# Interleaving two narrow projections with their neighbours, folding the squares of four norms, and moving work in two attention stages of a two-block transformer on one core

## The chip, the cores and the metric

The kernel runs on one core of one Trainium2 chip. The metric is the device time of the whole program in microseconds, the median of several runs. The engines of the core are written as in the profile: PE (TensorE), DVE (VectorE), ACT (ScalarE), POOL (GpSimd) and SP (SyncE, which here issues the DMAs of the weights).

## The reference

Batch 1, 256 positions, width 1024. The first block has two layers. Cut to what matters here, layer 1 is

```python
hk = rmsnorm(x, kv_norm_g)
kvf = hk @ kvf_w                                    # keys 1024, values 1024, 16 forget gates
k, v = kvf[..., :D], kvf[..., D:2 * D]
log_f = log_sigmoid(kvf[..., 2 * D:] + fgate_b)
c_bhs = cumsum(log_f, axis=1)
x = x + fox_attention(rmsnorm(x, norm_mix_g[1]), w_q, w_o, k, v, c_bhs)
x = x + memory_cross_attention(rmsnorm(x, norm_mem_g[1]), mem_n, ...)
x = x + square(relu(rmsnorm(x, norm_ff_g[1]) @ ff_w1)) @ ff_w2
```

and the second block (`mod = silu(c) @ w_ada + b_ada`, a product with a 1024 x 9216 matrix, gives its nine shifts, scales and gates) is

```python
u = modulate(rmsnorm(h, norm_ff1), sh1, sc1)
h = h + 0.5 * g1 * ((silu(u @ w_gate) * (u @ w_up)) @ w_down)
u = modulate(rmsnorm(h, norm_mix), sh2, sc2)
gq, gk, gv, glr, gog, mq, mk, mv, ga, gb = split(u @ w_in)      # glr is 16 wide
log_a = log_sigmoid(glr @ w_gla_lr + b_gla_lr) / 16
y_a = (rmsnorm(gla_chunked(gq, gk, gv, log_a)) * silu(gog)) @ w_br_gla
y_b = moba_attention(mq, mk, mv, rel_bias) @ w_br_moba
h = h + g2 * ((sigmoid(ga) * y_a + sigmoid(gb) * y_b) @ w_out)
# then a second gated feed-forward, and a last rmsnorm
```

## The kernel before

Everything is held transposed: `x` is 8 tiles (kt) of 128 features by 256 positions, taken in 4 pairs p. Every product with a weight matrix is a **stage** of **chunks** (the table in `plan`), mostly 1024 x 256 of weights. A value is split into a high half (rounded) and a low half (the rest), and each product is high x high, low x high and high x low, so a tile pair costs a matmul 128x512 (L452) and one 128x256 (L454).

Each chunk goes round a ring of 4 slots: SP loads it to `raw`, ACT writes its high half (`split_hi`, L1062) 4 chunks ahead, DVE its low half (`split_lo`, L1588) 3 chunks ahead, PE multiplies into one of two accumulators `acc`, ACT copies the low part out (`low`, L1072), DVE adds it (`total`, L1602). PE may start a chunk when both halves of its weights are there (`weights_ready`) and the chunk two before it is summed (`acc_free`). The order on every engine is written by hand: each engine's block calls the same stages, and `leads` and `between` put chunks among the heads of an attention.

**Norms.** After a residual stage (`residual` on PE and ACT, `add_to_x` on DVE) ACT squares each pair of `x` into `aux` (two slots, L1109, the last pair tile by tile, L1198), PE sums over the partitions with a matrix of ones (`norm_sums`, L666), ACT and DVE make the root (L1124, L1126, then L1746 to L1750), DVE scales the tiles (L1801), ACT rounds them (L1144 or L1153) and DVE makes the low half (L1774, L1775, L1788). Behind the last sums PE runs 10 and 40 matmuls on constants (`keep_clock`, L684). In `memq0`, `ff0` and `ff1` the root is multiplied in later; there DVE writes the operand for the last two tiles itself (L1703, low halves L1709).

**Narrow stages.** `foxf` (16 forget gates) and `inlr` (16 columns) have the operand as weights and 16 columns to stream: 32 matmuls of 128x32 (L587) and 128x16 (L591). `foxf` stands between `foxk0` and `foxv0`; `inlr` stands first behind the norm `mixn`, ahead of `incols`. DVE makes the operand `hB` of the queries behind `hA` of the keys. The 16 columns of `inlr` are turned behind the first chunk of `incols` (L976), multiplied with `wlr` behind the second (L984), and `level_spans(0)` follows the fourth (L921).

**The modulation** is computed on DVE, not on PE: 72 **ada tiles** (L1947, two parts of 256 KB each), one behind each chunk named in `ADA_STAGES`. The next tile is loaded when this one is read.

**The mixing attention** (`moba`, 4 heads) has the gate chunks 3 and 4 in `leads` and 5, 6, 7 behind heads 0, 1, 2. DVE finishes `o_gla` (`gla_gate`, L2210, L2212) behind head 1, ACT and DVE split it into `hA` (L1548, L2217) behind head 3, and the `branch` stage (L491 to L493) reads that first.

## Time and profile before

| | |
|---|---|
| median of 3 runs | 1500.7 us (1500.23 to 1503.94) |
| the profiled execution's own time | 1500.1 us |
| its span in the trace | 1498.3 us |
| PE busy | 1464.4 us (98%) |
| PE weight loads busy | 1277.3 us (85%) |
| DVE busy | 1088.0 us (73%) |
| ACT busy | 682.6 us (46%) |
| mean granted clock of PE | 0.991 |

Busy times of an engine are the union of its instructions; PE's counts the filler matmuls too. Times in the trace count from the start of the span. A line of the timeline has start, duration, engine, line, operation, output <- inputs, shapes, count, and in brackets the idle time before it with what ended it.

### The profile page before, as it was taken

The numbers are of one execution on the slowest core, as the hardware profiler recorded it, in microseconds if no ns is written. First come the engines' busy times: TensorE is split into PE (matmuls) and PEld (weight loads), VectorE is DVE, ScalarE is ACT, GpSimd is POOL, SyncE is SP. The second block draws the span as 40 slices with busy tenths as digits, with TensorE's granted clock in tenths as the row PEclk, the third lists the DMA queues.
The fourth block names the chain that finished last, engine by engine and source line by source line (L and its number), as shares of the span: only waits on it lengthen the run. The fifth ranks groups of instructions, "written<-read, shape, count | busy, mean of one in ns | idle before, by whom it ended". The sixth has DMA issues, their size and how long they took to land.

```text
span 1498.3 us, 21849 instructions
## 1 busy us (share of the span) xinstructions
PE 1464.4 (98%) x8588; PEld 1277.3 (85%) x8588; DVE 1088.0 (73%) x1630; ACT 682.6 (46%) x891; POOL 31.5 (2%) x20
## 2 busy tenths in 40 slices
PE   7999999999999999999999999999999999999997
PEld 6878888888889777888888998878888888888887
DVE  3799356698777666557887669998568768798754
ACT  2223255455334444545554345554444356455542
POOL 0000000000000000000000000000005200000000
PEclk9999999999999999999999999999989999999999
DMA  8544433355675434434557747767554435466451
GB/s 325 191 158 163 161 127 141 113 194 194 249 264 201 154 119 167 141 113 141 196 196 263 269 167 282 268 224 258 209 187 153 143 118 183 169 253 216 146 175 66
DMA packets 60191, 279.31 MB, mean 186 GB/s; under 512 B 6632, under 2 KB 8105, under 8 KB 35274
## 3 DMA queue, kind: packets, MB, share of 16 engines
q1 hardware_dynamic: 55672, 266.49, 51.0%
q10 hardware_dynamic: 4434, 11.64, 2.2%
q8 instruction: 58, 0.95, 0.2%
q14 instruction: 27, 0.22, 0.0%
HBM read 273.89 MB, written 4.19 MB: 186 GB/s over the span
## 4 chain that ended last, share of the span: by engine, by line
PE 84%; DVE 10%; DMA 3%; ACT 2%; issue 1%; DVEq 0%; SPq 0%; ACTq 0%
PE acc L452 34%; PE acc L454 17%; PE acc L473 10%; DVE wsplit L1588 3%; PE acc L491 3%; PE acc L492 3%; PE acc L493 3%; DMA ada_w<-in_ada 3%; PE stat L666 3%; PE acc L587 2%; DVE ada_w L1947 2%; PE stat L772 2%; PE score L734 1%; PE acc L591 1%; DVE tsum L1602 1%
## 5 line engine op out<-in xcount | busy, mean ns | idle before, releaser
L452 PE MATMUL acc<-hA,wsplit 128*128 128x512 f32 x1664 | 592.5, 401 | 3.9 <-DVE tsum L1602 2.4
L454 PE MATMUL acc<-hA,wsplit 128*128 128x256 f32 x1664 | 465.6, 280 | 0.0
L1062 ACT ACTIVATE wsplit<-raw 128x2048 fp32r<-128x2048 f32 (+2 forms) x206 | 365.9, 1777 | 200.5 <-PE acc L454 157.2
L1588 DVE TENSOR_TENSOR wsplit<-raw,wsplit 128x2048 fp32r<-128x2048 f32 (+2 forms) x206 | 436.7, 2123 | 13.7 <-ACT wsplit L1062 13.7
L452 PEld LDWEIGHTS acc<-hA,wsplit 128*128 128x128 f32 x1664 | 313.5, 188 | 83.2 <-issue 4.6
L454 PEld LDWEIGHTS acc<-hA,wsplit 128*128 128x128 f32 x1664 | 314.7, 189 | 0.4
L452 PE MATMUL acc<-hid,wsplit 128*128 128x512 f32 x648 | 226.7, 392 | 0.0
L454 PE MATMUL acc<-hid,wsplit 128*128 128x256 f32 x648 | 182.7, 282 | 0.0
L1072 ACT ACTIVATE lowp<-acc 128x512 f32<-128x512 f32 x118 | 69.0, 585 | 200.8 <-PE acc L454 172.5
L452 PEld LDWEIGHTS acc<-hid,wsplit 128*128 128x128 f32 x648 | 121.7, 188 | 25.5
L454 PEld LDWEIGHTS acc<-hid,wsplit 128*128 128x128 f32 x648 | 122.5, 189 | 0.2
L1983 DVE SCALAR_TENSOR_TENSOR conv<-upad,taps,conv 128x256 f32<-128x256 f32 x240 | 98.2, 480 | 0.8
L1947 DVE CUSTOM_DVE_ANT_0 ada_w<-ada_w,cact,cols 128x512 f32<-128x512 f32 x72 | 54.9, 763 | 43.7 <-DMA ada_w<-in_ada 43.4
L1947 DVE CUSTOM_DVE_ANT_0 ada_w<-ada_w,cact,mod 128x512 f32<-128x512 f32 x72 | 54.9, 762 | 16.0 <-DMA ada_w<-in_ada 6.7
L491 PE MATMUL acc<-hid,wsplit 128*128 128x256 f32 x216 | 61.0, 283 | 0.0
L1280 ACT ACTIVATE prob<-score,small 128x256 f32<-128x256 f32 x56 | 26.0, 469 | 75.8 <-DVE small L1898 75.8
L587 PE MATMUL acc<-wsplit,hA 128*128 128x512 f32 (+1 forms) x160 | 58.1, 398 | 2.4 <-DVE hA L1775 1.9
L492 PE MATMUL acc<-hid,wsplit 128*128 128x256 f32 x216 | 60.3, 279 | 0.0
L493 PE MATMUL acc<-hid,wsplit 128*128 128x256 f32 x216 | 60.3, 279 | 0.0
L1598 DVE TENSOR_TENSOR tsum<-acc,lowp 128x512 f32<-128x512 f32 x40 | 27.6, 690 | 40.2 <-ACT lowp L1072 39.9
L473 PE MATMUL acc<-mem_h,raw 128*128 128x256 f32 x256 | 56.5, 380 | 0.0
L666 PE MATMUL stat<-aux,ones 128*128 128x256 f32 x176 | 46.6, 391 | 9.8 <-ACT aux L1109 9.7
(287 smaller groups left out, 2112.3 us busy)
## 6 DMA issues: line engine op xcount, KB each, us to landing
raw<-in_gu SPq DMA_DIRECT2D x44, 1024.0 KB, 4.9
ada_w<-in_ada SPq DMA_DIRECT2D x144, 256.0 KB, 4.7
raw<-in_up SPq DMA_DIRECT2D x32, 1024.0 KB, 4.9
raw<-in_down SPq DMA_DIRECT2D x32, 1024.0 KB, 4.9
raw<-in_dn SPq DMA_DIRECT2D x32, 704.0 KB, 4.1
raw<-in_pw SPq DMA_DIRECT2D x8, 1024.0 KB, 6.1
raw<-in_memk SPq DMA_DIRECT2D x8, 1024.0 KB, 4.8
raw<-in_memv SPq DMA_DIRECT2D x8, 1024.0 KB, 5.3
```

The source lines that it names most:

```text
L452: nc.tensor.matmul(dst.rearrange("p (s t) -> p s t", s=2), w, h, start=start, stop=False, skip_group_check=True)
L454: return nc.tensor.matmul(dst[:, 0:T], lo_w, h[:, 0, :], start=False, stop=stop, skip_group_check=True)
L473: mm = nc.tensor.matmul(acc[:, par, j, 0:T], lhs, rhs, start=kt == 0, stop=kt == KT - 1)
L491: nc.tensor.matmul(dst, w, h[:, 0, :], start=start, stop=False, skip_group_check=True)
L492: nc.tensor.matmul(dst, w, h[:, 1, :], start=False, stop=False, skip_group_check=True)
L493: return nc.tensor.matmul(dst, lo_w, h[:, 0, :], start=False, stop=stop, skip_group_check=True)
L587: nc.tensor.matmul(dst.rearrange("p (s n) -> p s n", s=2), h(kt)[:, 0, tt * P:(tt + 1) * P], w[:, :, kt * n:(kt + 1) * n], start=kt == 0, ...
L666: mm = nc.tensor.matmul(stat[:, 0, :], ones[:], aux[:, p % 2, j, :], start=p == 0 and j == 0, stop=p == PAIRS - 1 and j == 1, skip_group_c ...
L1062: nc.scalar.activation(wsplit[:, slot, 0, 0:elems_of(n)], raw[:, slot, 0:elems_of(n)], ACT.Copy).then_inc(S("w_hi"), 1)
L1588: V.tensor_tensor(wsplit[:, slot, 1, 0:e], src, wsplit[:, slot, 0, 0:e].bitcast(F32), ALU.subtract).then_inc(S("w_lo"), 1)
L1947: V.tensor_tensor_reduce(w, w, cact[:, half * HALF:(half + 1) * HALF], 1.0, mod[:, m:m + 1] if half else col("ada_b", m), ALU.mult, ALU.ad ...
L1983: ins = V.scalar_tensor_tensor(out=conv[:, kt, :], in0=u, scalar=w, in1=conv[:, kt, :], op0=ALU.mult, op1=ALU.add)
```

## The change

- **Plan.** The first chunk of `incols` becomes a stage of its own, `incol0`, ahead of `inlr`; `incols` has 7 chunks. The ada tile behind `foxv3` goes to chunk 6 of `dn1`, the one behind the old first `incols` chunk to chunk 3 of `ingates`.
- **Orders.** PE goes pair by pair: two tiles of `foxk0`, the same two of `foxf`, and so on; likewise `incol0` and `inlr`. On DVE and ACT pairs 0 and 1 of `hB` stay ahead of the sum of the keys, pairs 2 and 3 go behind the sum of the gates. The splits that belonged to `foxk0`, `foxf` and `foxv0` are moved back: DVE makes one behind `logf_ready` and two behind `negc_ready`. The last split for `foxo` goes from behind `foxv3` (head 10) to behind head 12. The turn of `inlr`'s result goes into the middle of the first chunk of `incols`, and what hung on chunk 1, 2, 3 of `incols` hangs on the same columns, now chunks 0, 1, 2.
- **Folded squares.** For `fox`, `mixn`, `ffb` and `final2` DVE adds the squares of pairs 0, 1 and 2 (two additions 128x512), and PE sums one folded pair and the last: 4 instead of 8 products with ones.
- **Last gate chunk.** Gate chunk 7 is cut in two halves of its depth, behind heads 2 and 3. `gla_gate` and `gla_hi` go behind head 2, `gla_lo` ahead of chunk 7's sum, and they write a tile of their own, `gl`.
- **Last low halves** (`memq0`, `ff0`, `ff1`): DVE writes both tiles first and both low halves after them; ACT rounds both before it squares.

```diff
@@ plan, ADA_STAGES
-        Stage("inlr", "rows16", 1, KT * 16), Stage("incols", "cols", 8, full),
+        Stage("incol0", "cols", 1, full), Stage("inlr", "rows16", 1, KT * 16), Stage("incols", "cols", 7, full),
-ADA_STAGES = [..., ("foxv3", range(1)), ..., ("dn1", range(6)), ("incols", range(4)), ("ingates", (1, 2)), ...]
+ADA_STAGES = [..., ("dn1", range(7)), ("incols", range(3)), ("ingates", (1, 2, 3)), ...]
@@ PE: norm_sums, residual
+                first = LAST - 1 if name in FOLDED else 0
                 for p in pairs:
+                    if p < first:
+                        continue
...
+                    if name in FOLDED and p == first:
+                        pe.wait_ge(S("squares_folded"), fold_count(name, 2))
...
+                    if norm in FOLDED and per > 1:
+                        if c == LAST * per + 1:
+                            early.extend(range(LAST))
+                            norm_sums(norm, early)
@@ PE: key projections, first mixing chunk, gate chunk 7
-            fox_chunk("k0")(0, 0)
-            linear("foxf", hA, None)
+            for p in range(PAIRS):
+                fox_chunk("k0")(0, 0, pair=p)
+                fox_gates(0, 0, pair=p)
-            linear("inlr", hA, pair_ready(norm_base("mixn")))
+            for p in range(PAIRS):
+                in_col(0, 0, pair=p)
+                in_lr(0, 0, pair=p)
...
+            in_chunk(0, 0, 0)
+            turn_lr()
+            in_chunk(0, 0, 1)
...
-                      between={h: (lambda c=h + 5: gate_chunk(c, c)) for h in range(3)})
+                      between={0: lambda: gate_chunk(5, 5), 1: lambda: gate_chunk(6, 6),
+                               2: lambda: gate_chunk(7, 7, span=([4, 5, 6, 7], True, False)),
+                               3: lambda: gate_chunk(7, 7, span=([0, 1, 2, 3], False, True))})
@@ DVE: add_to_x
+                    if norm_name in FOLDED and known in (2 * st.per_acc, 3 * st.per_acc):
+                        p = known // st.per_acc - 1
+                        wait("norm_sq", PAIRS * norm_index(norm_name) + p + 1)
+                        if p == 2:
+                            wait("squares_folded", fold_count(norm_name, 1))
+                        V.tensor_tensor(aux[:, 1, :, :], aux[:, 1, :, :], aux[:, 0, :, :],
+                                        ALU.add).then_inc(S("squares_folded"), 1)
@@ DVE: key projections, moba
-                if name == "v3":
-                    split_lo(STAGE["foxo"], 3, 3)
+            fox_queries([0, 1])
+            fox_chunk("k0", split=False)
+            linear("foxf", ..., width=HEADS, split=False)
...
+            fox_queries([2, 3])
...
+            split_lo(STAGE["foxk0"], AHEAD, AHEAD)
+            fox_chunk("v0", split=False)
...
+            for name in ("foxf", "foxv0"):
+                split_lo(STAGE[name], AHEAD, AHEAD)
...
-                      between={0: lambda: (gate_chunk(5, 5), gla_newton()), 1: lambda: (gate_chunk(6, 6), gla_gate()),
-                               2: lambda: gate_chunk(7, 7), 3: gla_lo})
+                      between={0: lambda: (gate_chunk(5, 5), gla_newton()), 1: lambda: gate_chunk(6, 6),
+                               2: gla_gate, 3: lambda: (gla_lo(), gate_chunk(7, 7))})
```

How the instructions stand, at three places. On **PE at the key projections**, the end of `foxk0` and the start of `foxf` before (their other rows read the same):

```order
L452 MATMUL acc<-hA,wsplit 128x512
L454 MATMUL acc<-hA,wsplit 128x256
L452 MATMUL acc<-hA,wsplit 128x512
L454 MATMUL acc<-hA,wsplit 128x256
L587 MATMUL acc<-wsplit,hA 128x32
L591 MATMUL acc<-wsplit,hA 128x16
L587 MATMUL acc<-wsplit,hA 128x32
L591 MATMUL acc<-wsplit,hA 128x16
```

and now, from the end of a pair of `foxk0` over the same pair of `foxf` to the next pair:

```order
L474 MATMUL acc<-hA,wsplit 128x512
L476 MATMUL acc<-hA,wsplit 128x256
L613 MATMUL acc<-wsplit,hA 128x32
L617 MATMUL acc<-wsplit,hA 128x16
L613 MATMUL acc<-wsplit,hA 128x32
L617 MATMUL acc<-wsplit,hA 128x16
L613 MATMUL acc<-wsplit,hA 128x32
L617 MATMUL acc<-wsplit,hA 128x16
L613 MATMUL acc<-wsplit,hA 128x32
L617 MATMUL acc<-wsplit,hA 128x16
L474 MATMUL acc<-hA,wsplit 128x512
L476 MATMUL acc<-hA,wsplit 128x256
```

The 32 narrow matmuls stood together before and now stand in four groups of 8, each behind 8 wide ones (16 instructions of the two lines in a pair).

On **DVE at the key projections** before (`fk`, `small`, `fv` are the sums of keys, gates and values, `wsplit` a `split_lo`, L2067 and L2069 the gates, L2075 to L2082 the cumulative sums):

```order
L1788 TENSOR_TENSOR hB<-tsum,hB 128x2x256 x2
L1602 TENSOR_TENSOR fk<-acc,lowp 128x512
L1588 TENSOR_TENSOR wsplit<-raw,wsplit 128x2048
L1602 TENSOR_TENSOR small<-acc,lowp 128x32
L1588 TENSOR_TENSOR wsplit<-raw,wsplit 128x2048
L2067 TENSOR_TENSOR small<-small,cols 128x32
L2069 SCALAR_TENSOR_TENSOR small<-small 128x32
L1602 TENSOR_TENSOR fv<-acc,lowp 128x2x256
L1588 TENSOR_TENSOR wsplit<-raw,wsplit 128x2048
```

and now:

```order
L1664 TENSOR_TENSOR small<-acc,lowp 128x32
L2144 TENSOR_TENSOR small<-small,cols 128x32
L1874 SCALAR_TENSOR_TENSOR tsum<-x,cols,rstd 128x256 x2
L1861 TENSOR_TENSOR hB<-tsum,hB 128x2x256
L1874 SCALAR_TENSOR_TENSOR tsum<-x,cols,rstd 128x256 x2
L1861 TENSOR_TENSOR hB<-tsum,hB 128x2x256 x2
L2147 SCALAR_TENSOR_TENSOR small<-small 128x32
L1650 TENSOR_TENSOR wsplit<-raw,wsplit 128x2048
L1664 TENSOR_TENSOR fv<-acc,lowp 128x2x256
```

The sums of keys and gates come ahead of half of `hB` and of all splits; the first split follows the gates, two more follow the cumulative sums.

On **DVE at heads 1 to 3 of the mixing attention** before:

```order
L1602 TENSOR_TENSOR gates<-acc,lowp 128x512
L1588 TENSOR_TENSOR wsplit<-raw,wsplit 128x1024
L2210 TENSOR_TENSOR o_gla<-o_gla,aux 128x1024
L2212 SCALAR_TENSOR_TENSOR o_gla<-o_gla,cols,inT 128x1024
L1911 TENSOR_TENSOR mo<-stat,mo 128x256
L1903 RECIPROCAL small<-small 128x2
```

and now:

```order
L1664 TENSOR_TENSOR gates<-acc,lowp 128x512
L1650 TENSOR_TENSOR wsplit<-raw,wsplit 128x1024
L1985 TENSOR_TENSOR mo<-stat,mo 128x256
L1977 RECIPROCAL small<-small 128x2
L1979 TENSOR_TENSOR prob_122<-prob_122,small 128x512
L2295 TENSOR_TENSOR o_gla<-o_gla,aux 128x1024
L2297 SCALAR_TENSOR_TENSOR o_gla<-o_gla,cols,inT 128x1024
L1985 TENSOR_TENSOR hA<-stat,hA 128x256
L2302 TENSOR_TENSOR gl<-o_gla,gl 128x4x256
L1664 TENSOR_TENSOR gates<-acc,lowp 128x512
```

The two passes over `o_gla` now follow the last head's probabilities, and the low half `gl` comes ahead of the last gate sum.

## Rows read from the trace of the kernel before

**Rows 1.** Waits of PE, summed by line (total us, times, longest us).

```profile
PE stat L666 <- ACT aux L1109: 9.7, 2, 8.3
PE acc L452 <- DVE tsum L1602: 2.4, 3, 1.2
```

**Rows 2.** Stretches: busy us (count) of PE, PEld, DVE, ACT, POOL; PEclk, DMA share, GB/s.

```profile
482.70:485.68 2.98, 2.98 (x30) 2.98 (x28) 2.91 (x6) 1.22 (x3) 0.00 (x0) 1.00 0.00 0
485.68:492.51 6.83, 6.37 (x22) 5.53 (x22) 5.94 (x7) 4.98 (x8) 0.00 (x0) 0.50 0.45 146
594.91:598.32 3.41, 3.41 (x16) 3.30 (x16) 1.96 (x5) 1.70 (x8) 0.00 (x0) 0.50 0.53 214
1086.43:1096.67 10.24, 10.22 (x40) 9.45 (x41) 5.20 (x9) 2.90 (x4) 0.00 (x0) 0.50 0.43 142
1243.44:1246.85 3.41, 3.17 (x13) 2.77 (x13) 1.64 (x2) 2.23 (x3) 0.00 (x0) 0.50 0.47 154
```

**Rows 3.** Timeline of PE: products with ones in `out`, then a wait for squares in `dn1`.

```profile
1291.82 2.32 PE L666 MATMUL stat<-aux,ones 128*128 128x256 f32 x10
1293.98 1.25 PE L684 MATMUL turned<-mask_bf,ident_bf 128*128 128x256 bf16 x10
...
1032.12 1.13 PE L666 MATMUL stat<-aux,ones 128*128 128x256 f32 x4 [1.42 <-ACT aux L1109]
```

**Rows 4.** Timeline of PE at the key projections.

```profile
475.91 0.48 PE L452 MATMUL acc<-hA,wsplit 128*128 128x512 f32 x1
...
487.27 0.77 PE L587 MATMUL acc<-wsplit,hA 128*128 128x512 f32 x1 [0.46 <-DVE fk L1602]
...
496.40 0.50 PE L452 MATMUL acc<-hB,wsplit 128*128 128x512 f32 x1
505.08 0.27 PE L875 MATMUL score<-mask_bf,ident_bf 128*128 128x256 bf16 x1
```

**Rows 5.** Timeline of DVE at the key projections.

```profile
487.04 2.28 DVE L1588 TENSOR_TENSOR wsplit<-raw,wsplit 128x2048 fp32r<-128x2048 f32 x1
```

**Rows 6.** Timeline of DVE, then PE, behind `foxv3` (heads 10 and 11).

```profile
589.41 0.75 DVE L1947 CUSTOM_DVE_ANT_0 ada_w<-ada_w,cact,mod 128x512 f32<-128x512 f32 x1
590.09 2.29 DVE L1588 TENSOR_TENSOR wsplit<-raw,wsplit 128x2048 fp32r<-128x2048 f32 x1
593.23 0.55 PE L754 MATMUL turned<-ident,prob 128*128 128x128 f32 x3 [1.84 <-DVE prob L1905]
```

**Rows 7.** Timeline of PE at `inlr` and the first `incols` chunk.

```profile
1083.50 0.25 PE L587 MATMUL acc<-wsplit,hA 128*128 128x32 f32 x1
1086.45 0.39 PE L587 MATMUL acc<-wsplit,hA 128*128 128x32 f32 x1 [1.93 <-DVE hA L1775]
1091.59 0.77 PE L452 MATMUL acc<-hA,wsplit 128*128 128x512 f32 x1
1099.69 0.48 PE L452 MATMUL acc<-hA,wsplit 128*128 128x512 f32 x1
1118.29 1.16 PE L921 MATMUL turned<-spans,loga 128*128 128x128 f32 x8
```

**Rows 8.** Timeline of DVE, then PE, at heads 2 and 3 of the mixing attention.

```profile
1238.29 1.28 DVE L2212 SCALAR_TENSOR_TENSOR o_gla<-o_gla,cols,inT 128x1024 f32<-128x1024 f32 x1
1243.18 1.38 PE L772 MATMUL stat<-probT,inV 128*128 128x256 f32 x4 [1.87 <-DVE hA L1911]
1244.80 0.55 PE L491 MATMUL acc<-hA,wsplit 128*128 128x256 f32 x1 [0.24 <-DVE hA L2217]
```

**Rows 9.** Timeline of DVE, then PE, at the last low half of `ff0`.

```profile
289.52 0.42 DVE L1709 TENSOR_TENSOR hA<-tsum,hA 128x256 fp32r<-128x256 f32 x1 [0.48 <-ACT hA L1191]
291.93 0.58 PE L452 MATMUL acc<-hA,wsplit 128*128 128x512 f32 x1
```

**Rows 10.** Waits of DVE for the ada tiles; then a stretch of `dn1` (columns as rows 2).

```profile
DVE ada_w L1947 <- DMA ada_w<-in_ada: 50.1, 39, 3.6
...
1028.40:1044.70 16.30, 14.88 (x85) 12.96 (x84) 13.43 (x24) 4.66 (x4) 0.00 (x0) 1.00 0.82 276
```

More of the change, by code:

```diff
@@ L153, with square_at, fold_count, stat_count @@
 TILED_OPERANDS = ["memq0", "ff0", "ff1"]
+FOLLOWS = {"pw2": "memq0", "memo0": "ff0", "down0": "fox", "foxo": "memq1", "memo1": "ff1", "down1": "ffa",
+           "dn1": "mixn", "out": "ffb", "dn2": "final2"}
+FOLDED = ["fox", "mixn", "ffb", "final2"]
+def square_at(name, p):
+    return 0 if name in FOLDED and p == LAST else p % 2
+def fold_count(name, n):
+    return 2 * FOLDED.index(name) + n
+def stat_count(q):
+    return sum(2 if n in FOLDED else PAIRS for n, _ in NORMS[:q])
 LN_TABLE = 3
@@ L540, in body @@
                     begins, ends = half in (None, 0), half in (None, 1)
+                    if pair is not None:
+                        kt_all, begins, ends = [2 * pair, 2 * pair + 1], pair == 0, pair == PAIRS - 1
+                    if span is not None:
+                        kt_all, begins, ends = span
                     if st.per_acc == 1:
@@ L1009, in behind_mixing @@
                 return after
-            linear("incols", hA, None, after=behind_incols)
+            _, in_chunk = linear("incols", hA, None, after=behind_incols, steps=True)
+            in_chunk(0, 0, 0)
+            turn_lr()
+            in_chunk(0, 0, 1)
+            for c in range(1, STAGE["incols"].chunks):
+                in_chunk(c, c)
             linear("inrows", hA, None, after=behind_mixing("inrows"))
@@ L1087, in body @@
                         post(known // st.per_acc, known // st.per_acc)
-                    if st.base + known + RING < N_CHUNKS and not (late and known == st.chunks - 1):
+                    if st.base + known + RING < N_CHUNKS and split and not (late and known == st.chunks - 1):
                         split_hi(st, c + RING, known + RING)
@@ L1793, in lo @@
                     last.then_inc(S("norm_lo"), 1)
-                for p in range(PAIRS):
+                for p in pairs:
                     if which or p >= 2:
@@ L2083, in _ @@
                             ALU.subtract).then_inc(S("negc_ready"), 1)
+            for name in ("foxf", "foxv0"):
+                split_lo(STAGE[name], AHEAD, AHEAD)
             fox_chunk("q0")
@@ L2276, in wait @@
                 pool.wait_ge(S(sem), value)
[L2278 removed]
+            wait("acc_summed", STAGE["incols"].acc_base + 3)
             for i in range(NL + 1):
```

157 lines of the change are left out of this document (90 added, 67 removed).

## Prediction

> **What bounds the kernel now.** I read the shares of the engines first: PE is busy for 98% of the span, so the time is PE's, and only three things can shorten it: less work on PE, fewer waits of PE, and a higher clock. The list of PE's waits comes next [rows 1]; outside the start of the program it holds a few microseconds, and the first line's 9.7 us are 8.3 us of start and one wait of 1.4 us. Then the stretches in which the granted clock is 0.50, that is 1.2 instead of 2.4 GHz [rows 2]. There are four inside the program, 6.83 + 3.41 + 10.24 + 3.41 = 23.9 us, and since PE does half its work there, they cost half of that, 12 us. They count as busy, so the share of busy time hides them. The reader should see in the first line of rows 2 what came before the first of them: PE was busy for all of 2.98 us, on the narrow matmuls of `foxf`.
>
> A difference under 0.3%, 4.5 us, is what a measurement of this kernel can hardly tell from none.
>
> **The change, part by part.**
>
> *Folded squares.* Ten products with ones take from 1291.82 to 1293.98, 0.216 us each, and a pair has four such instructions: 0.86 us [rows 3]. Four norms lose two pairs each: 4 x 2 x 0.86 = 6.9 us of PE, in stages where PE never idles, all of it on the path. In `dn1` the first product also waited 1.42 us for squares that DVE's lateness held up [rows 3]; its place in the order is gone, and the folded one comes ten chunks of slack later: 1.4 us. DVE gains 8 additions of 128x512, about 0.7 us each like its other passes of that shape (priced at 0 for the path: a fold stands between splits that are three chunks ahead). Uncovered, they would cost 8 x 0.7 = 5.5 us. Sum 8.3 us.
>
> *Key projections.* Before, `foxk0` starts at 475.91, `foxv0` at 487.27, `foxq0` at 496.40, the first scores at 505.08 [rows 4]. From 496.40 to 505.08 lie a chunk and a half, 24 couples of wide matmuls, 0.36 us each: 1.4 us for a pair's four, 5.7 us a chunk. Narrow ones come every 0.11 us (27 in 2.98 us, the row's other records being ends of wide ones [rows 2]), 0.9 us for a pair's eight. The narrow work also covers the time for which pair 1 is late today: from 475.9, 4 x 2.3 = 9.2 us give 485.1. `foxv0` then needs the keys' sum, which now stands ahead of half of `hB`; ACT's copy and DVE's addition, 0.7 us each behind the last wide pair, put it at 486.0. At full clock `foxv0` ends at 491.7. Next late is DVE: half of `hB` and the gates (some 4 us, an estimate from passes of 0.7 us and ACT's between them), and only then the split of 2.28 us [rows 5] that `foxq0` needs, which ends near 492.8. `foxq0` runs 492.8 to 498.6; the two further splits end at 497.5 and 499.9 and are hidden; the first scores start at 501.4. That is 505.1 - 501.4 = 3.7 us, taken as 3.6. Bounds: the clock stays low as now, and a gain of 0.2 us is left; or no wait at the sum and 4.3 us.
>
> *Behind `foxv3`.* The ada tile and the split stand between the sum and head 12's probabilities; without their 3.9 us (two passes of 0.75 with their reads, and 2.29) PE's wait of 1.84 us [rows 6] goes. The half-clocked stretch of 3.41 us that begins right behind this wait and the small matmuls after it [rows 2] should go too, 1.7 us. Sum 3.5 us. The split is put at 0 behind head 12, where DVE has a gap before its next scores. The tile's new place in `dn1` is free as long as DVE keeps up: there it is busy for 13.43 of 16.3 us [rows 10], and has room after them.
>
> *First mixing chunk.* Today `inlr` starts at 1083.50, waits 1.93 us in the middle, and `incols` chunk 1 starts at 1099.69 [rows 7], 10.24 us of this at half clock [rows 2]. Interleaved: 4 x 2.3 us of work plus about 0.6 us of waiting for pair 1 give 1093.3, and a wait of 0.5 us for the accumulator 1093.8. Old chunk 1 then runs with the turn inside it and ends with the logits 6.9 us later at 1100.7; today that is 1099.69 + 6.9 = 1106.6. From there the order is the same and all moves up by 5.9 us; the loga chain on DVE and ACT ends near 1112.3, when PE is at 1112.1 in place of 1118.29. I take 6.0 us. Bounds: 0.9 us with the clock as low as today, 7 us with nothing waiting.
>
> *Mixing attention.* `gla_gate` (2.5 us [rows 8]) leaves the road of head 3's probabilities, and half a gate chunk, 2.9 us, covers it. But `gla_hi` now stands ahead of head 2's output on ACT, and head 3's values wait for that: PE idles about 1.1 us instead of 1.86, and the branch starts at 1244.0 instead of 1244.80. With a full clock there [rows 2] 1.0 us more are gained behind it: 1.8 us, bounds -0.5 and 2.5. The ada tile added to gate chunk 3 delays head 0's probabilities by 1.7 us, which just fits under gate chunk 4: 0, and 1.7 us if uncovered.
>
> *Last low halves.* The second low half of `ff0` ends at 289.94, PE takes up its chunks behind the sums at 291.93 [rows 9]. What is earlier on DVE was already early enough: 0 (bounds 0 and 0.3 for each of three).
>
> Sum: 8.3 + 3.6 + 3.5 + 6.0 + 1.8 = 23.2 us. The new order leaves short waits and narrow groups, and at one of these places I expect one stretch of 3.41 us at half clock, 1.7 us: 21.5 us. Against the profiled execution's own 1500.1 us this gives 1478.6 us; the median of the runs is 0.6 us higher, so 1479.
>
> The row on the clock is worth weighing against a rule. The row: the clock fell behind 2.98 us in which PE idled for none [rows 2]. The Trainium skill ("TensorE: Matmul & The Clock Gate", section "Why this matters for your kernels") names idle gaps between bursts of matmuls as what lowers the clock in the middle of a kernel. By that rule the mixing of narrow and wide matmuls would gain nothing on the clock, and the waits that stay would lower it again: 13.0 us saved in place of 21.5, the first rival below. The trace is against the rule at `foxf`, and with it at the two other places where PE had idled for 1.8 us or more.
>
> **Rivals.**
>
> 1. *The clock falls as often as now at the three rebuilt places.* For it: narrow groups of 0.9 us remain, next to waits of 0.5 to 1.1 us. Against it: 1.42 us of waiting in `dn1` did not lower it (PEclk 1.00 [rows 10]). The key projections give back 3.4, the mixing chunk 5.1, the attention 1.7 us: 23.2 - 10.2 = 13.0 us, 1487 us. In this case the reorder does not do what it is built for, and what is left is the sums and the waits.
> 2. *DVE's postponed splits become PE's wait.* Three splits of 2.28 us [rows 5] are made later than now, and `foxq0` waits for the first with only 0.1 us to spare by my count. If all three lie bare, 6.8 us: 21.5 - 6.8 = 14.7 us, 1485 us. Against it: the second and third have a whole chunk in front of them.
> 3. *Slower: DVE sets the pace of `dn1`.* A chunk there takes PE 3.9 us; DVE needs 1.6 for the split, 1.7 for an ada tile, and waits for the tile's load, 3.6 us at worst [rows 10]. If every one of the seven tiles waits that long, PE loses 3.0 us a chunk, 21 us, and with the folds' 5.5 us ahead of splits it is 26.5 against 23.2 saved: 1503 us. It turns the sign only if the loads are late by more than 3.1 us on average; the mean now is 50.1 / 39 = 1.3 us, and PE's whole waiting on DVE's sums is 2.4 us [rows 1].
>
> **How the numbers follow.** Forecast 0.72, rival 1 0.15, rival 2 0.09, rival 3 0.02, and 0.02 for a smaller gain that is within 4.5 us. Forecast with its unknowns (no low stretch 1477, upper bounds of the terms 1475, two low stretches 1480, attention and splits at the poor ends 1483) reaches from 1475 to 1483; rivals 1 and 2 lie at 1485 to 1487. The range 1474 to 1487 leaves out less than 2 in 10. All cases but the last two are faster by over 4.5 us: faster 0.96, same 0.02, slower 0.02.
>
> **What would show it.** 144 products with ones instead of 176, and no wait ahead of them in `dn1`. No stretch of clock 0.50 from the start of `foxk0` to the first scores, at most one at `incol0`. First scores 25.5 us behind the first matmul of `foxk0` (29.2 now). No wait of PE for probabilities behind `foxv3`. `level_spans(0)` 28.7 us behind the first matmul on the operand of `mixn` (34.8 now). The wait ahead of head 3's values near 1.1 us. The forecast is wrong if the half-clocked time stays over 15 us, if PE waits for a split at `foxq0` or `foxk1` by more than 1 us, or if DVE's waits for ada tiles grow past 60 us.

## The result and the profile after

| | before | after |
|---|---|---|
| median of the runs, us | 1501.76 (4 runs) | 1480.69 (4 runs, 1479.62 to 1482.45) |
| profiled execution: own time and span, us | 1500.1; 1498.3 | 1481.0; 1478.9 |
| PE busy, us | 1464.4 | 1446.7 |
| time at half clock before PE's last instruction, us | 23.9 | 0 |

The ratio is 0.9862, with a 95% interval from 0.985 to 0.9874: 21.1 us faster. The forecast was 1479.0, within 1474 to 1487.

The page of the changed kernel: PE's share, and its clock in 40 slices.

```profile
PE 1446.7 (98%) x8556; PEld 1261.6 (85%) x8556; DVE 1092.1 (74%) x1638; ACT 682.5 (46%) x891; POOL 31.5 (2%) x20
PEclk9999999999999999999999999999999999999999
```

PE is still what the time is made of. Its busy time fell by 17.7 us, where 6.9 us of products and 12 us of half clock make 18.9. The products with ones, from the view of their line:

```profile
L698 PE MATMUL stat<-aux,ones x144: 377/379/766, 8.2 to 1470.9; 128*128 128x256 f32 x144
```

PE's waits by line (us in total, times, longest), as [rows 1]:

```profile
PE stat L698 <- ACT aux L1161: 8.2, 1, 8.2
PE acc L474 <- DVE tsum L1664: 4.8, 6, 1.4
...
PE acc L474 <- issue: 1.6, 1, 1.6
PE stat L808 <- DVE hA L1985: 1.0, 1, 1.0
```

The first line has lost its second wait, the one in `dn1`. The second has grown from 2.4 to 4.8 us, and the third is new. So the waits that were attacked are gone or shorter (head 3's values wait 1.0 us in place of 1.9), except the one at `foxv0`, which grew from 0.46 to 0.71 us. And DVE has made others.

The timeline of PE, as [rows 4, 6, 7, 8]:

```profile
474.22 0.48 PE L474 MATMUL acc<-hA,wsplit 128*128 128x512 f32 x1
484.35 0.47 PE L613 MATMUL acc<-wsplit,hA 128*128 128x512 f32 x1 [0.71 <-DVE fk L1664]
491.14 0.50 PE L474 MATMUL acc<-hB,wsplit 128*128 128x512 f32 x1
499.58 0.28 PE L913 MATMUL score<-mask_bf,ident_bf 128*128 128x256 bf16 x1
585.80 0.55 PE L790 MATMUL turned<-ident,prob 128*128 128x128 f32 x3
1073.39 0.47 PE L474 MATMUL acc<-hA,wsplit 128*128 128x512 f32 x1
1076.35 0.50 PE L474 MATMUL acc<-hA,wsplit 128*128 128x512 f32 x1 [0.54 <-DVE hA L1848]
1084.12 0.47 PE L474 MATMUL acc<-hA,wsplit 128*128 128x512 f32 x1 [0.71 <-DVE inT L1664]
1102.87 1.16 PE L963 MATMUL turned<-spans,loga 128*128 128x128 f32 x8
1227.27 0.89 PE L808 MATMUL stat<-probT,inV 128*128 128x256 f32 x4 [1.04 <-DVE hA L1985]
1228.40 0.36 PE L513 MATMUL acc<-gl,wsplit 128*128 128x256 f32 x1 [0.24 <-DVE gl L2302]
```

The first scores stand 25.36 us behind the first matmul of `foxk0` (29.17 before), `level_spans(0)` 29.48 us behind the first matmul on the operand of `mixn` (34.79 before), and the matmul at 585.80 waits for nothing. The same places as stretches, columns as [rows 2]:

```profile
477.39:483.64 6.25, 6.25 (x46) 5.70 (x44) 3.65 (x9) 2.50 (x4) 0.00 (x0) 1.00 0.16 42
483.64:499.58 15.94, 15.23 (x85) 12.54 (x84) 14.76 (x22) 9.87 (x12) 0.00 (x0) 1.00 0.40 136
580.00:605.00 25.00, 24.42 (x175) 19.86 (x174) 12.29 (x21) 8.84 (x23) 0.00 (x0) 1.00 0.38 126
1073.39:1083.41 10.02, 9.48 (x67) 8.59 (x64) 5.66 (x15) 3.37 (x8) 0.00 (x0) 1.00 0.40 137
1226.22:1250.00 23.78, 22.50 (x189) 22.31 (x189) 20.55 (x30) 19.00 (x27) 0.00 (x0) 1.00 0.62 222
```

The granted clock is 1.00 in all five. The new waits stand in `dn1` and in `gu2`. The timeline of DVE in `dn1`, then of PE there and in `gu2`:

```profile
1037.85 0.75 DVE L2021 CUSTOM_DVE_ANT_0 ada_w<-ada_w,cact,cols 128x512 f32<-128x512 f32 x1 [1.68 <-DMA ada_w<-in_ada]
1039.43 1.78 DVE L1738 SCALAR_TENSOR_TENSOR x<-acc,mod,x 128x256 f32<-128x256 f32 x4
1041.13 1.61 DVE L1650 TENSOR_TENSOR wsplit<-raw,wsplit 128x1408 fp32r<-128x1408 f32 x1
...
1042.84 0.47 PE L474 MATMUL acc<-hid,wsplit 128*128 128x512 f32 x1 [1.62 <-issue]
1320.61 0.50 PE L474 MATMUL acc<-hA,wsplit 128*128 128x512 f32 x1 [0.91 <-DVE tsum L1664]
1327.76 0.50 PE L474 MATMUL acc<-hA,wsplit 128*128 128x512 f32 x1 [1.23 <-DVE tsum L1664]
```

The releaser "issue" does not name what PE waited for; DVE's rows do: the seventh tile waits 1.68 us for its load, the group of `x` comes behind it, and the split that PE stands for ends at 1042.74, 0.1 us before PE goes on.

Matching the same instruction in both traces, stage by stage, gives where the 19.4 us went (PE's last instruction ends 19.4 us earlier):

| stretch | forecast | measured |
|---|---|---|
| products with ones, four norms | 6.9 | 6.9 (1.72 each) |
| the wait for squares in `dn1` | 1.4 | 1.4 |
| key projections (`foxk0` to first scores) | 3.6 | 3.8 |
| behind `foxv3` | 3.5 | 3.5 (1.9 of wait, 1.5 of clock) |
| first mixing chunk | 6.0 | 5.3 |
| mixing attention and branch | 1.8 | 2.3 (1.0 and 1.3) |
| last low halves | 0 | 0 |
| one stretch at half clock | -1.7 | none |
| PE waits for DVE in `dn1` | 0 | -1.6 |
| `gu2` takes 126.68 us instead of 124.62 | 0 | -2.1 |
| `gu1` takes 128.28 us instead of 127.48 | 0 | -0.8 |
| small differences elsewhere | 0 | 0.7 |
| sum | 21.5 | 19.4 |

### The profile page after: what moved, and what is told of

Read it like the earlier page. It is cut to its first block, busy times and chain, and to the rows that moved or that the text cites. A ratio compares the mean times of both kernels' runs of the same rounds, so it can differ in the third digit from the quotient of the medians.

```text
span 1478.9 us, 21797 instructions
## 1 busy us (share of the span) xinstructions
PE 1446.7 (98%) x8556; PEld 1261.6 (85%) x8556; DVE 1092.1 (74%) x1638; ACT 682.5 (46%) x891; POOL 31.5 (2%) x20
## 4 chain that ended last, share of the span: by engine, by line
PE 84%; DVE 8%; DMA 5%; ACT 2%; issue 1%; DVEq 0%; SPq 0%; ACTq 0%
PE acc L474 33%; PE acc L476 17%; PE acc L495 10%; DMA ada_w<-in_ada 5%; PE acc L513 3%; PE acc L514 3%; PE acc L515 3%; DVE wsplit L1650 3%; PE acc L613 2%; PE stat L698 2%; DVE ada_w L2021 2%; PE stat L808 2%; PE score L770 2%; PE acc L617 1%; PE turned L716 1%
## 5 line engine op out<-in xcount | busy, mean ns | idle before, releaser
L1112 ACT ACTIVATE wsplit<-raw 128x2048 fp32r<-128x2048 f32 (+3 forms) x206 | 365.8, 1777 | 191.5 <-PE acc L476 147.0
L1650 DVE TENSOR_TENSOR wsplit<-raw,wsplit 128x2048 fp32r<-128x2048 f32 (+3 forms) x206 | 436.9, 2123 | 7.5 <-ACT wsplit L1112 7.4
L1122 ACT ACTIVATE lowp<-acc 128x512 f32<-128x512 f32 (+1 forms) x118 | 69.0, 585 | 188.5 <-PE acc L476 164.4
L495 PE MATMUL acc<-raw,mem_h 128*128 128x256 f32 x256 | 55.8, 379 | 0.0
L495 PEld LDWEIGHTS acc<-mem_h,raw 128*128 128x128 f32 x256 | 48.4, 190 | 8.7 <-issue 2.3
```

Source lines behind the costliest of these rows:

```text
L495: mm = nc.tensor.matmul(acc[:, par, j, 0:T], lhs, rhs, start=kt == 0, stop=kt == KT - 1)
L1112: nc.scalar.activation(wsplit[:, slot, 0, 0:elems_of(n)], raw[:, slot, 0:elems_of(n)], ACT.Copy).then_inc(S("w_hi"), 1)
L1122: last = nc.scalar.activation(lowp[:, :, 0:width], acc[:, par, :, width:2 * width], ACT.Copy)
L1650: V.tensor_tensor(wsplit[:, slot, 1, 0:e], src, wsplit[:, slot, 0, 0:e].bitcast(F32), ALU.subtract).then_inc(S("w_lo"), 1)
```

## The experiments

Two questions were left. Is it the block of narrow matmuls or PE's idle time that brings the clock down? And do the new waits behind DVE belong to the change, and can they be avoided? The single runs of one kernel differ by 2 to 9 us, so where a term is smaller than that I read it from the trace, between the same two instructions, and not from the median.

### Narrow matmuls in one block

```diff
             for p in range(PAIRS):
                 fox_chunk("k0")(0, 0, pair=p)
+            for p in range(PAIRS):
                 fox_gates(0, 0, pair=p)
```

The same edit at `in_col` and `in_lr`.

> The changed kernel with the narrow matmuls in one block again: all of foxk0, then all of foxf; all of incol0, then all of inlr. Everything else stays. Theory (the block of narrow matmuls by itself brings the clock down, without any idle time of PE): a stretch at 0.50 begins behind foxf, and one behind inlr, of 3.4 to 10 us each, though PE idles no more than 0.8 us next to them; with the second pair of columns waited for again (0.6 us at each place) the time is 1485 to 1490 us against 1481 for the changed kernel. Rival (idle gaps alone bring it down): the clock stays at 1.00 at both places, and only the waits of 0.6 us come back: 1482 to 1483 us.

Measured: 1484.33 us, ratio 0.9884 (0.9868 to 0.9901). Stretches of this kernel, columns as [rows 2]:

```profile
480.60:483.54 2.94, 2.94 (x30) 2.94 (x28) 0.69 (x1) 0.66 (x2) 0.00 (x0) 1.00 0.31 89
483.54:490.37 6.83, 6.83 (x25) 5.97 (x25) 5.19 (x11) 3.73 (x7) 0.00 (x0) 0.50 0.01 2
1080.07:1087.65 7.58, 7.53 (x52) 6.71 (x52) 4.90 (x9) 3.30 (x4) 0.00 (x0) 1.00 0.43 149
1087.65:1094.48 6.83, 6.83 (x26) 5.90 (x26) 3.18 (x3) 2.00 (x2) 0.00 (x0) 0.50 0.68 236
```

The first line is `foxf` alone, up to the fall: PE is busy for all of it, and with its last five matmuls the clock falls for 6.83 us, as it did in the kernel before. PE's last wait ahead of it, 0.70 us, ended at 476.16, 7.4 us before the fall. At `inlr` the clock falls too, but this place is less clean: PE waited 1.33 us ahead of 1080.07, more than the 0.8 us that I had allowed. The first scores come 28.58 us behind `foxk0` and `level_spans(0)` 32.97 us behind the operand, 3.2 and 3.5 us later than in the changed kernel. The median is 3.6 us up, a little under what I had written; of the 6.7 us that the two places lose, 2.1 are given back in `gu2`, which happened to have no wait in this trace. The theory holds: at `foxf` a block of matmuls of 16 and 32 columns comes with a fall though PE is busy throughout, and mixing them into the wide ones is what stops it. The other traces agree. In the three of kernels with the block (this one and two of the kernel before) the clock falls at both places; in the eleven with the mixed order it falls at neither.

### An idle time among wide matmuls

```diff
                 def after(c):
+                    if name == "dn1" and c == 11:
+                        pe.wait_ge(S("acc_summed"), STAGE["dn1"].acc_base + 3)
                     if norm in FOLDED and per > 1:
```

> The changed kernel with one wait more: in dn1 PE does not begin chunk 12 before DVE has added the third group to x, so that it idles in the middle of wide matmuls about as long as it did ahead of the two low stretches of the kernel before (1.84 and 1.87 us). Theory (idle time of this length does not lower the clock where the matmuls around it are wide): PE idles 1.8 to 2.0 us, the clock stays at 1.00 behind it, and the time grows by 0.3 to 2 us (some of it is taken off the wait that dn1 has anyway). Rival (idle gaps lower the clock): a stretch of 3.41 us at 0.50 follows within some microseconds, 1.7 us more: 3.5 us in all.

Measured: 1481.58 us, ratio 0.9874 (0.9857 to 0.989). The wait in the timeline of PE:

```profile
1052.16 0.38 PE L513 MATMUL acc<-hid,wsplit 128*128 128x256 f32 x1 [1.88 <-DVE x L1740]
```

The stretches ahead of it and behind it, columns as [rows 2]:

```profile
1041.00:1052.16 11.16, 7.87 (x45) 6.76 (x45) 8.32 (x10) 5.77 (x6) 0.00 (x0) 1.00 0.72 254
1052.16:1075.10 22.94, 22.90 (x190) 21.75 (x191) 12.46 (x17) 10.57 (x13) 0.00 (x0) 1.00 0.64 222
```

Two waits, 1.44 and 1.88 us, within 11 us, and the clock stays at 1.00. The 0.9 us more in the median are within the runs' scatter. In this one trace, among wide matmuls, idle time of this length cost only itself; the other waits of that length are counted under the last heading.

### Without folding

```diff
-FOLDED = ["fox", "mixn", "ffb", "final2"]
+FOLDED = []
```

> The changed kernel without folding: the list of the folded norms is empty, so all 176 products with ones are made, at their old places. Theory (the term of the forecast): PE's products add 4 x 2 x 0.86 = 6.9 us, and the product in dn1 waits for squares again, 1.4 us: 8.3 us more than the changed kernel, 1489 us. Rival (DVE's 8 additions and the waits for tiles in dn1 took part of it): without the additions of 0.7 us DVE is earlier, the wait of 1.61 us at 1041 shrinks, and only 5.5 to 7 us come back, 1487 to 1488 us.

Measured: 1488.96 us, ratio 0.9918 (0.9901 to 0.9934), 8.3 us over the changed kernel, which is the term. That the medians hit it is in part chance, because in the trace it is made up otherwise than I had it: in `dn1` PE waits for squares twice, 1.68 and 3.08 us, and at the second wait the clock falls, so that from the start of `dn1` to the first matmul on `mixn`'s operand 8.0 us are lost where the forecast has 3.1 (1.7 of products and 1.4 of wait). The wait in the timeline of PE:

```profile
1043.81 2.07 PE L698 MATMUL stat<-aux,ones 128*128 128x256 f32 x4 [3.08 <-ACT aux L1161]
```

The stretch at half clock:

```profile
1042.92:1049.75 6.83, 5.94 (x17) 5.00 (x18) 4.78 (x4) 1.90 (x2) 0.00 (x0) 0.50 0.63 200
```

So folding is worth more than its products in a `dn1` with seven tiles: with it PE no longer stands for squares that DVE's lateness holds up. Part of what it costs to undo it was offset by the wait in `gu2` (2.1 us), absent here.

### The old order of ACT and DVE at the key projections

```diff
-            fox_queries([0, 1])
-            fox_chunk("k0", split=False)
+            fox_queries([0, 1, 2, 3])
+            fox_chunk("k0")
```

`foxf` and `foxv0` likewise, and ACT to match.

> The changed kernel with the old order on ACT and DVE at the key projections (all of hB ahead of the sums of foxk0 and foxf, each split behind its own sum), the interleaved matmuls on PE kept. Theory (the order of DVE is what frees foxv0): the keys' sum comes 1.0 to 1.5 us later behind the first matmul of foxk0, PE's wait of 0.71 us at foxv0 grows to 1.7 to 2.2 us, and the time by 1.0 to 1.5 us: the first scores start 26.4 to 26.9 us behind foxk0 instead of 25.36. Rival (the interleaving alone brought the 3.8 us): 25.4 us, no difference.

Measured: 1480.25 us, ratio 0.9859 (0.9843 to 0.9876). PE's wait for the keys' sum:

```profile
485.41 0.47 PE L613 MATMUL acc<-wsplit,hA 128*128 128x512 f32 x1 [1.95 <-DVE fk L1659]
```

The first scores stand 27.01 us behind `foxk0` instead of 25.36: the order on ACT and DVE is worth 1.65 us, a little over the 1.0 to 1.5 that I had written. Of that 1.24 us are the longer wait at `foxv0`, and 0.26 a new one ahead of the scores. The median does not show it. In this trace PE waited 2.77 us in `dn1` (1.62 in the changed kernel's) and not at all in `gu2` (2.14). That the rival is wrong rests on the trace between the two instructions, not on the medians. The clock, as a stretch over this wait and what follows it, is 1.00:

```profile
483.00:500.00 17.00, 15.05 (x86) 12.50 (x86) 12.68 (x18) 9.86 (x12) 0.00 (x0) 1.00 0.56 203
```

So behind the mixed narrow matmuls even a wait of 1.95 us came with no fall.

### The tile back behind `foxv3`

```diff
-ADA_STAGES = [("down0", range(15)), ("foxv1", range(1)), ("foxv2", range(1)), ("down1", range(15)),
-              ("gu1", range(19)), ("dn1", range(7)), ("incols", range(3)), ("ingates", (1, 2, 3)), ("gu2", range(8))]
+ADA_STAGES = [("down0", range(15)), ("foxv1", range(1)), ("foxv2", range(1)), ("foxv3", range(1)), ("down1", range(15)),
+              ("gu1", range(19)), ("dn1", range(6)), ("incols", range(3)), ("ingates", (1, 2, 3)), ("gu2", range(8))]
```

and `split_lo(STAGE["foxo"], 3, 3)` behind `foxv3`'s sum instead of behind head 12.

> The changed kernel with one ada tile behind foxv3 again (six in dn1 in place of seven) and the split of foxo's chunk 3 behind foxv3's sum. Theory (the forecast's term, and the seventh tile is what PE waits for in dn1): PE waits 1.8 us for probabilities behind foxv3 and a stretch of 3.4 us at 0.50 follows, so that from the first scores to head 13's values it takes 94.4 us instead of 90.98; in dn1 the wait of 1.4 to 2.8 us for a split goes below 0.5 us. Together 1.0 to 2.0 us slower than the changed kernel. Rival 1 (the wait in dn1 has another cause, such as the folds): it stays at 1.4 us or more and the time is 3.5 us longer. Rival 2 (that wait behind foxv3 no longer lowers the clock): only 1.8 us come back there, and the time is the changed kernel's.

Measured: 1478.56 us, ratio 0.9843 (0.9826 to 0.986). The timeline of PE behind `foxv3`:

```profile
587.68 0.55 PE L790 MATMUL turned<-ident,prob 128*128 128x128 f32 x3 [1.84 <-DVE prob L1979]
```

The stretch there, and that of `dn1` with the norm behind it:

```profile
585.84:602.00 16.16, 13.74 (x94) 10.47 (x93) 7.39 (x17) 5.57 (x18) 0.00 (x0) 1.00 0.33 135
1005.00:1073.00 68.00, 67.95 (x448) 61.46 (x447) 48.56 (x73) 30.76 (x31) 0.00 (x0) 1.00 0.73 249
```

Three things. The wait is back to the hundredth (1.84, [rows 6]), and this stretch takes 1.9 us more. The low stretch is not back: rival 2 is right there, and the clock's fall behind `foxv3` did not hang on this wait alone. And PE idles 0.05 us in the 68 us of `dn1`, with the folds in place: PE's wait there comes with the seventh tile in a row. Moving that tile took 1.9 us from one stage and gave 1.4 to 2.8 to another, so this part of the change, as it was made, brought nothing on balance by the traces. The median without it is 2.1 us lower than that of the changed kernel, but the intervals overlap, and this trace has 3.1 us of waits in `gu2`: no difference is shown.

### Gate chunk 7 in one piece

```diff
-                               2: lambda: gate_chunk(7, 7, span=([4, 5, 6, 7], True, False)),
-                               3: lambda: gate_chunk(7, 7, span=([0, 1, 2, 3], False, True))})
+                               2: lambda: gate_chunk(7, 7)})
```

with `gla_gate`, `gla_hi` and `gla_lo` where they stood before.

> The changed kernel with gate chunk 7 in one piece ahead of head 2's values and gla_gate behind gate chunk 6, gla_lo behind gate chunk 7, as before; the tile of its own for the gla output is kept. Theory (the forecast's term): PE waits 1.8 to 1.9 us ahead of head 3's values instead of 1.05, the branch begins 126.5 us behind level_spans(0) instead of 125.53, and a stretch of 3.41 us at 0.50 comes back in the branch (1.3 to 1.7 us): 2.3 to 2.7 us slower than the changed kernel. Rival (half a chunk in front is worth nothing, because gla_hi ahead of head 2's output costs what it gains): 125.5 us to the branch, and the same time.

Measured: 1484.99 us, ratio 0.988 (0.9859 to 0.9901). The timeline of PE at head 3's values:

```profile
1229.59 1.03 PE L808 MATMUL stat<-probT,inV 128*128 128x256 f32 x4 [1.87 <-DVE hA L1984]
```

The stretch behind:

```profile
1230.20:1237.03 6.83, 6.24 (x30) 5.98 (x29) 1.61 (x3) 2.57 (x4) 0.00 (x0) 0.50 0.22 72
```

The wait is back (1.87), and the branch starts 126.51 us behind `level_spans(0)`, as before; in the changed kernel it is 125.53. The low stretch is back too, and twice as long as before. Together the part is worth 3.7 us in this trace, 1.0 of it the wait and 2.7 the clock. The median is 4.3 us up, where I had written 2.3 to 2.7, and cannot be read as this part's worth: the trace also has waits of 0.9 to 1.2 us four times in `gu2`, and one of 1.61 us in `down0`.

### The low halves as before

```diff
-                        for low in range(2 * j):
+                        for low in (j,):
```

with ACT's copy and square of each tile in the old order.

> The changed kernel with the low half of the last pair's first tile made ahead of the second tile's operand again, on ACT and DVE. Theory (the forecast's term of 0): DVE and ACT have slack there, the stretches from memo0 and memo1 to the next operands keep their lengths to 0.1 us, and the time is the changed kernel's to 0.3%. Rival (0.3 us for each of the three norms): PE takes up its chunks behind the sums 0.2 to 0.4 us later at each, 0.6 to 1.0 us in all.

Measured: 1479.31 us, ratio 0.9849 (0.9833 to 0.9865). From the last products of `ff0` to the first matmul of `foxk0` it is 183.79 us (290.76 to 474.55), in the changed kernel 183.78 (290.44 to 474.22). Around the other two norms the stretches from PE's wait at 197.56 to the one at 252.14, and from the one at 652.17 to the first matmul of `gu1` at 874.88, differ from those of the changed kernel by 0.01 us. The term is 0, as forecast. This run too had a longer wait in `dn1`, 2.38 us, and a stretch of 3.41 us at half clock that begins 0.4 us before the wait ends.

### Both kernels once more

No edit.

> The kernel before, unchanged, for a second trace. Theory (each of its four stretches at 0.50 belongs to what PE does at that place): they are all there again, behind foxf, behind foxv3, at inlr and at the branch, 20 to 27 us in all. Rival (some of them hang on chance, as the one behind foxv3, which did not come back with its wait): one or more are missing or elsewhere, though the waits ahead of them, 1.84, 1.92 and 1.86 us, are there.

> The changed kernel, unchanged, for a second trace. Theory (the new waits of PE in dn1 belong to the change, those in gu2 to chance in when ada tiles land): PE waits 1.4 to 2.8 us for a split in dn1 again; in gu2 either 0 or 2 to 4 us; no stretch at 0.50 at the places that were rebuilt. Rival (both belong to the change): about 1.6 us in dn1 and 2.1 us in gu2, as in the first trace.

Measured: before 1499.65 us, after 1482.98 us. The kernel before has its four stretches at the same four places, with 3.4 us behind `foxf` in place of 6.83:

```profile
488.75:492.17 3.42, 3.42 (x12) 2.83 (x12) 3.42 (x3) 2.51 (x3) 0.00 (x0) 0.50 0.21 29
```

The places are the program's, the length is not. The changed kernel has none at the rebuilt places, and one in `dn1`. Its timeline of PE there:

```profile
1045.12 0.47 PE L474 MATMUL acc<-hid,wsplit 128*128 128x512 f32 x1 [2.44 <-issue]
```

And the stretch:

```profile
1046.38:1049.76 3.38, 3.38 (x13) 2.79 (x12) 3.38 (x3) 0.31 (x1) 0.00 (x0) 0.50 0.86 288
```

`gu2` has no wait in it. Over the nine traces of the changed kernel and the variants so far, PE waits in `dn1` for splits in all seven that have both the folds and the seventh tile (1.40 to 2.80 us), and in `gu2` in three of nine (2.1, 3.1 and 4.0 us). In the three traces with waits in `gu2`, DVE stands 4.0 to 6.4 us for tiles in that stage, in the six others 0.2 to 1.9 us. The wait in `dn1` is the change's; the one in `gu2` is not one that every execution has. The two traces of the kernel before have none there; two are too few to say whether the change makes it likelier.

### Tiles with gaps between them

```diff
-              ("gu1", range(19)), ("dn1", range(7)), ("incols", range(3)), ("ingates", (1, 2, 3)), ("gu2", range(8))]
+              ("gu1", range(19)), ("dn1", (0, 1, 3, 4, 6, 9, 10)), ("incols", range(3)), ("ingates", (1, 2, 3)), ("gu2", range(0, 16, 2))]
```

> The changed kernel with its ada tiles at other chunks of the same stages: in dn1 at chunks 0, 1, 3, 4, 6, 9, 10 instead of 0 to 6, in gu2 at the even chunks 0 to 14 instead of 0 to 7. Theory (DVE is late in dn1 because tiles in consecutive chunks wait for their loads, some 1.2 to 1.7 us each): with gaps between them the loads are there, DVE's waits for tiles fall by 8 us or more, PE's wait in dn1 (1.4 to 2.8 us) and those in gu2 (2.1 us where they occur) go, and the time falls by 1.5 to 3.5 us against the changed kernel, to 1477 to 1479 us. Rival (the loads of the weights are what is late in these stages): the waits stay, and the time with them, 1480 to 1481 us.

Measured: 1477.3 us (five runs, 1474.25 to 1478.5), ratio 0.9833 (0.9816 to 0.985). PE has no wait in `dn1` and none in `gu2`. DVE's waits for tiles fell from 58.1 to 49.2 us, but the second trace of the changed kernel has 51.9, so the sum proves little: one tile in `dn1` still waits 4.03 us, where nobody stands behind DVE. It is the place of the waits that counts, not their sum. The median is 3.4 us under the changed kernel's. Only the 1.4 to 2.8 us of `dn1` can be put down to the new places for sure, since the second trace of the changed kernel had no wait in `gu2` either.

### Two tiles fewer in `gu1`

```diff
-              ("gu1", range(19)), ("dn1", (0, 1, 3, 4, 6, 9, 10)), ("incols", range(3)), ("ingates", (1, 2, 3)), ("gu2", range(0, 16, 2))]
+              ("gu1", (*range(16), 21)), ("dn1", (0, 2, 4, 6, 8, 9, 10, 12, 13)), ("incols", range(3)), ("ingates", (1, 2, 3)), ("gu2", range(0, 16, 2))]
```

> The kernel with spread tiles, and of gu1's 19 tiles two go to dn1 and one to gu1's last chunk: gu1 has tiles at chunks 0 to 15 and 21, dn1 at 0, 2, 4, 6, 8, 9, 10, 12, 13, gu2 at the even ones 0 to 14. Theory (in gu1 the tiles at chunks 16 to 18 meet the passes for the norm there, and DVE falls behind): PE's waits for DVE's sums at the end of gu1, 1.35 + 0.57 + 0.52 = 2.4 us, fall below 0.7 us, none comes in dn1, and the time is 1474.8 to 1476.5 us. Rival (nine tiles and two folds are too much for DVE in dn1): gu1's waits go, but PE waits 1 us or more for a split in dn1, and the time stays at 1477 us.

Measured: 1477.08 us, ratio 0.9835 (0.9822 to 0.9849). The waits at the end of `gu1` are gone, all 2.4 us of them. A new one stands at the end of `dn1` (timeline of DVE, then PE):

```profile
1061.80 0.75 DVE L2021 CUSTOM_DVE_ANT_0 ada_w<-ada_w,cact,cols 128x512 f32<-128x512 f32 x1 [3.84 <-DMA ada_w<-in_ada]
...
1064.36 0.70 PE L698 MATMUL stat<-aux,ones 128*128 128x256 f32 x2 [1.83 <-ACT aux L1254]
```

The tile of chunk 13 stands ahead of the last addition to `x`, whose squares PE needs, and its load is late. Why, SP's timeline shows:

```profile
1054.20 0.33 SPq L409 DMA_DIRECT2D raw<-in_incols  x1
1054.88 1.23 SPq L429 DMA_DIRECT2D ada_w<-in_ada  x2
```

The tile's load is issued 0.7 us behind a load of 1 MB of the next stage's weights. The trace has both landing 6.9 us after their issue, the tile's first part 0.6 us behind the weights, where the tiles' loads in `dn1` of the changed kernel take 2.8 to 4.3 us. A stretch of 3.4 us at half clock follows PE's wait. What `gu1` gained is given back: the median is that of the run before. Of my rival the sense was right (too much in `dn1`), the place was not.

### The tile of chunk 13 at chunk 5

```diff
-              ("gu1", (*range(16), 21)), ("dn1", (0, 2, 4, 6, 8, 9, 10, 12, 13)), ("incols", range(3)), ("ingates", (1, 2, 3)), ("gu2", range(0, 16, 2))]
+              ("gu1", (*range(16), 21)), ("dn1", (0, 2, 4, 5, 6, 8, 9, 10, 12)), ("incols", range(3)), ("ingates", (1, 2, 3)), ("gu2", range(0, 16, 2))]
```

> The kernel of the run before with dn1's tiles at chunks 0, 2, 4, 5, 6, 8, 9, 10, 12: the one at chunk 13, whose load was 3.8 us late and held up the last addition to x, goes to chunk 5. Theory (nothing else of that wait): PE's wait of 1.82 us for the squares of the last tile goes, with the stretch of 3.4 us at 0.50 behind it, and no wait over 0.6 us is left in gu1, dn1 and gu2: 1473.5 to 1475.5 us. Rival (the load is late wherever the ninth tile stands): PE waits 1 us or more for a split or for squares in dn1 again, 1476 to 1478 us.

Measured: 1475.31 us (five runs, 1472.97 to 1476.5), ratio 0.9823 (0.981 to 0.9837). `gu1`, `dn1` and `gu2` as stretches, here and, in the same order, in the changed kernel:

```profile
873.00:1003.00 130.00, 129.70 (x737) 111.62 (x735) 118.14 (x199) 71.42 (x99) 0.00 (x0) 1.00 0.63 223
1003.00:1070.18 67.18, 66.00 (x440) 59.77 (x439) 51.74 (x85) 28.90 (x29) 0.00 (x0) 1.00 0.80 277
1278.00:1402.00 124.00, 124.00 (x703) 107.34 (x702) 98.13 (x148) 68.52 (x90) 0.00 (x0) 1.00 0.54 187
```

```profile
873.00:1003.00 130.00, 127.02 (x718) 108.58 (x717) 118.93 (x204) 69.00 (x94) 0.00 (x0) 1.00 0.65 229
1003.00:1073.39 70.39, 68.73 (x455) 62.12 (x455) 50.63 (x79) 31.10 (x32) 0.00 (x0) 1.00 0.74 253
1281.00:1407.00 126.00, 123.86 (x703) 106.94 (x702) 98.23 (x148) 67.67 (x90) 0.00 (x0) 1.00 0.54 185
```

PE idles 0.3, 1.2 and 0 us instead of 3.0, 1.7 and 2.1. Nearly all of the 1.2 us is one wait of 1.13 us ahead of the products with ones, for the second fold, which DVE makes late. I had not expected it: no wait over 0.6 us was to be left. This version beats both kernels: its interval lies wholly under that of the changed kernel (0.985 to 0.9874).

## Why the prediction was right

The six terms add up to 23.2 us measured, as forecast, though single ones are off by up to 0.7. The rest is luck: the 1.7 us that I took off for a low stretch were not lost, and PE's wait in `dn1`, which I had at nothing, took 1.6 instead. `gu2` and `gu1` then lost 2.9 us that no term had, and small differences gave 0.7 back. The time came out 1.7 us above the forecast.

*Folded squares.* Confirmed by the traces of both kernels: 144 products, 6.9 us, and 8.3 us with the wait. That DVE's 8 additions cost nothing on the path is not contradicted: `dn1` with the folds and six tiles keeps PE busy for 67.95 of 68.00 us. The wait of 1.13 us in the last version shows that this cover is thin.

*Key projections.* Confirmed in its times: the keys' sum let `foxv0` start 10.13 us behind `foxk0` (forecast 10.1), `foxq0` 16.92 us (forecast 16.9), the first scores 25.36 (forecast 25.5). One step was short: the last wide pair ends at 484.2 by my count, and two passes of 0.7 us give 485.6 for the sum, not the 486.0 that I wrote and that came. Without the mixing of the narrow matmuls 3.2 us are lost, without the order on ACT and DVE 1.65; together that is more than 3.8, so the two overlap.

*Behind `foxv3`.* The wait was as forecast. The clock's part, 1.7 us, was read as a result of this wait, and that step is not borne out: with the wait put back the clock stayed at 1.00. In both traces of the kernel before it fell there. The 1.5 us were gained, but what gained them I have not found.

*First mixing chunk.* 5.3 instead of 6.0: the accumulator's wait was 0.71 us and not 0.5, the mixed chunk took 0.2 us more, and from the logits to `level_spans(0)` it was 11.8 us where I counted 11.4. My count did not hold together here: if all moves up by 5.9 us, the old 11.7 us (1106.6 to 1118.29) stay. `level_spans(0)` stands 29.48 us behind the operand, 28.7 was written.

*Mixing attention.* 1.0 us of waiting and 1.3 of clock, forecast 0.8 and 1.0; the wait ahead of head 3's values was 1.04 (forecast 1.1). With gate chunk 7 in one piece both come back, and the low stretch is in all three traces that have the wait of 1.87 us there and in none of the eleven without.

*The stretch at half clock.* I put one at the rebuilt places. The first trace has none, the second has one, in `dn1`, behind a wait that I had not forecast.

*What was wrong.* "The tile's new place in `dn1` is free as long as DVE keeps up." DVE did not keep up. It had 13.43 us of work in 16.3 [rows 10], and that counted no wait for loads; seven tiles in consecutive chunks wait for their loads in most of them, and the last wait falls just ahead of a group of `x` and the split PE needs. The tiles spread over the stage show it from the other side: seven tiles, and no wait of PE's. This is the mechanism of the third rival, at 1.4 to 2.8 us where I had priced it only at its full 21 us. A bound between the two belonged in the sum. DVE's waits for tiles, 58.1 us, stayed just under the 60 at which I would have called the forecast wrong.

*The rivals.* I had counted rivals 1 and 2 without the 0.6 us between the profiled execution's sum and the median; with them they are 1487.7 and 1486.0 us. The first did not happen at the rebuilt places; with the narrow matmuls in one block again it does. The second did not happen: PE waits for no split at `foxq0` or `foxk1`. The third came at a tenth of its price.

*The rule on gaps.* The Trainium skill ("TensorE: Matmul & The Clock Gate", section "Why this matters for your kernels") puts the fall down to idle gaps, and it means gaps longer than nearly all waits in these traces. So the forecast used the rule more widely than it is written when it let waits of 0.5 to 1.1 us lower the clock, and counted in its favour places where PE had idled for 1.8 us (three of them, `inlr` with 1.93 us among them, not two). The runs bear the rule out only in part: at `foxf` the grouped kernel's clock fell with no gap at all, while in `dn1` gaps of 2.38, 2.44 and 3.08 us each came with a fall and one of 2.77 us did not.

## What to carry to other kernels

A term that moves work to an engine "with slack" needs the waits of that engine in it, not its busy time alone: count what stands behind each wait for a load, and whether another engine wants it. In this kernel it paid to leave gaps between the pieces of work that depend on a load, and to put none ahead of the last step of a stage. And where a short block of narrow matmuls brings TensorE's clock down, try mixing them into wide ones. Here the mixed order took no longer (9.4 us for `foxk0` with `foxf` and 10.0 for `incol0` with `inlr`, where the grouped kernel took 10.8 and 11.6, waits and half clock counted), and it kept the clock up in eleven of eleven traces.
